# Moving one projection's units into later stages, and a new opening and closing of an expert stage, in a two-block transformer kernel on Trainium2

## What is computed

```python
# first block, mixer
proj = h @ w_in                       # split in columns: fq fk fv f_logit nq kc vc ... merge_logit
k_cmp, v_cmp = compress_kv(kc, vc)    # blocks of 32 tokens, stride 16, a two-layer MLP with gelu
y_fox = fox_attention(fq, fk, fv, log_f)
y_nsa = nsa_attention(nq, k_cmp, v_cmp, k_slc, v_slc, k_win, v_win, gates)
g = sigmoid(merge_logit)              # (tokens, 2 branches, 1024)
up = einsum('bsnc,ncd->bsnd', stack([y_fox, y_nsa]), w_branch)
merged = sum(g * up, axis=2);  h = h + merged @ w_out
# then 128 retrieved experts per token ("PEER"), rmsnorm
# second block: a gated delta rule mixer, then 16 experts that each choose 32 tokens
probs = softmax(xn @ router_w);  gate, idx = top_k(probs.T, 32)
xg = xn[idx]
y = (silu(xg @ w_gate[e]) * (xg @ w_up[e])) @ w_down[e] * gate
out = rmsnorm(h + scatter_add(y, idx))
```

## Time and profile before

| | us |
|---|---|
| median of 3 runs (lowest to highest) | 2330.33 (2324.06 to 2330.75) |
| profiled execution, time | 2327.65 |
| profiled execution, span from first to last instruction | 2325.9 |
| mean granted TensorE clock | 0.831 of 2.4 GHz |

### The profile page before, as it was taken

How to read it: one execution, slowest core, us unless ns; L and a number is a source line. 1 busy time by engine, 2 the same in 40 slices (tenths; PEclk the granted TensorE clock), 3 DMA queues, 4 the chain that set the end, 5 groups by cost and what they waited for, 6 DMA issues and landing times. The chain is left out here.

```text
span 2325.9 us, 22733 instructions
## 1 busy us (share of the span) xinstructions
PE 1733.6 (75%) x8678; PEld 871.0 (37%) x8678; DVE 756.1 (33%) x1643; ACT 438.6 (19%) x915; POOL 288.9 (12%) x297
## 2 busy tenths in 40 slices
PE   6997887987877778859788867666666666666675
PEld 6975687433333333329687631111111111111111
DVE  3425327876767666543464220000000000000001
ACT  4414223222212222224411020000000000000000
POOL 0000002433343333400051000000000000000000
PEclk9987998999899998989888777777777777787777
DMA  5530248999999999965000369999999999999996
GB/s 205 179 132 17 73 138 330 420 420 420 420 420 420 420 420 420 420 256 211 1 1 1 127 253 420 420 421 420 421 420 421 420 421 420 420 420 420 421 420 273
DMA packets 111080, 738.63 MB, mean 318 GB/s; under 512 B 13856, under 2 KB 15136, under 8 KB 27040
## 3 DMA queue, kind: packets, MB, share of 16 engines
q1 hardware_dynamic: 73856, 469.14, 50.0%
q0 software_dynamic: 36864, 268.45, 27.8%
q10 hardware_dynamic: 288, 0.08, 0.0%
HBM read 736.58 MB, written 1.05 MB: 317 GB/s over the span
## 5 line engine op out<-in xcount | busy, mean ns | idle before, releaser
L886 PE MATMUL ps<-arena 128*128 128x512 f32 x768 | 390.1, 661 | 132.0 <-ACT arena L947 132.0
L1898 PE MATMUL ps<-arena,xe 128*32 128x512 f32 x2048 | 353.7, 792 | 169.0 <-DMA arena<-in_experts_in 168.8
L1944 DVE TENSOR_TENSOR low<-low,ps 128x512 f32<-128x512 f32 x16 | 11.0, 687 | 890.4 <-PE ps L1898 890.4
L886 PEld LDWEIGHTS ps<-arena 128*128 128x128 f32 x768 | 156.0, 209 | 357.6 <-issue 188.6
L1030 DVE CUSTOM_DVE_ANT_0 arena<-arena,ps 128x1024 f32<-128x1024 f32 x192 | 231.9, 1218 | 113.5 <-DMA arena<-in_peer,arena 109.0
L833 POOL DMA_INDIRECT arena<-in_peer,arena x192 | 182.0, 948 | 692.8 <-DVE arena L1022 364.7
L1912 PE MATMUL ps<-arena,hT 128*32 128x512 f32 x1024 | 182.0, 811 | 102.2 <-DMA arena<-in_experts_down 90.5
L1898 PEld LDWEIGHTS ps<-arena,xe 128*32 128x32 f32 x2048 | 50.5, 122 | 461.7 <-DMA arena<-in_experts_in 419.6
L1912 PEld LDWEIGHTS ps<-arena,hT 128*32 128x32 f32 x1024 | 26.2, 127 | 240.5 <-DMA arena<-in_experts_down 213.3
L947 ACT ACTIVATE arena<-ident,arena 128x128 f32<-128x128 f32 x256 | 81.8, 390 | 122.1 <-DVE arena L1039 120.6
L333 PE MATMUL ps<-first_h_parts,first_w_parts 128*128 128x256 f32 x816 | 100.3, 286 | 5.3 <-DVE first_h_parts L298 4.3
(11 more groups left out here) (352 smaller groups left out, 1984.1 us busy)
## 6 DMA issues: line engine op xcount, KB each, us to landing
arena<-in_experts_in SPq DMA_DIRECT2D x256, 1024.0 KB, 26.9
arena<-in_experts_down SPq DMA_DIRECT2D x128, 1024.0 KB, 26.9
ring<-in_stream SPq DMA_DIRECT2D x80, 512.0 KB, 3.5
arena<-in_stream SPq DMA_DIRECT2D x14, 1024.0 KB, 7.5
arena<-in_peer,arena POOLq DMA_INDIRECT x192, 27.1
h<-in_x SPq DMA_DIRECT2D x1, 1024.0 KB, 5.1
arena<-in_sel SPq DMA_DIRECT2D x1, 1024.0 KB, 5.7
arena<-in_subkeys SPq DMA_DIRECT2D x2, 512.0 KB, 5.0
```

The source lines that it names most:

```text
L886: last = nc.tensor.matmul(ps[:, 4 + 2 * t + half, :], diag[:, n % DIAGS, :], slot(n)[:, D + half * BANK:D + (half + 1) * BANK], start=firs ...
L1898: last = nc.tensor.matmul(ps[32 * j:32 * (j + 1), 4 + r // KB, :], xe[:, k, :], w[:, j * BANK:(j + 1) * BANK], start=(k == 0), stop=(k == ...
```

## The change

**Merge gates.** The group of 16 units leaves the projection. The stream of weights after the projection is now mixed (`MIXED`): the eight compression pieces c0 to c7 and the 16 gate pieces m0 to m15. Six gate units run in the compression stage, between its pieces, and ten in attention, one in each of the steps 0, 1, 3, 4, 6, 7, 9, 10, 12 and 13, right behind the scores. ACT still makes the high parts, GpSimd instead of DVE makes the low parts, and two units share PSUM bank 7, from which ACT copies the pair (`gate_keep`) before the next pair may start. The Sigmoid comes in the merge block, eight activations on ACT. To free bank 7, the values of attention and of the compression's second layer move into bank 6. DVE has no gate unit's work any more.

```diff
-G_CMP, G_BRANCH, G_OUT, G_WQ, G_PEER = 40, 48, 56, 64, 80
+MIXED = ("c0 c1 m0 c2 c3 m1 c4 c5 m2 c6 c7 m3 m4 m5 m6 m7 m8 m9 m10 m11 m12 m13 m14 m15").split()
+G_MIXED, G_BRANCH, G_OUT, G_WQ, G_PEER = 24, 48, 56, 64, 80
+G_CMP = [G_MIXED + MIXED.index(f"c{i}") for i in range(8)]
+G_GATE = [G_MIXED + MIXED.index(f"m{i}") for i in range(16)]
+EARLY_GATES = 6
+G_ATT = G_GATE[EARLY_GATES]
...
     front(T, "mix", 0, ring, 0, [("F", 9, pieces(proj, 0, 9), ACT.Copy),
-                                 ("F", 8, pieces(proj, 9, 17), ACT.Sigmoid),
                                  ("T", 3, vdst, ACT.Copy)], small, refill, xs=T.arena[:, -NT * D:].rearrange("p (t d) -> p t d", t=NT))
...
+    def gate_split_high(act, u):
+
+        ring.arrived(act, G_GATE[u])
+        if u >= 2:
+            act.wait_ge(gate_done, u - 1)
+        nc.scalar.activation(gate_parts(u)[0], gate_raw(u), ACT.Copy).then_inc(gate_high, 1)
+
+    def gate_split_low(pool, u):
+
+        pool.wait_ge(gate_high, u + 1)
+        high, low = gate_parts(u)
+        nc.gpsimd.tensor_tensor(low, gate_raw(u), high.bitcast(F32), ALU.subtract).then_inc(gate_low, 1)
+
+    def gate_unit(pe, u):
+
+        if u >= 2 and u % 2 == 0:
+            pe.wait_ge(gate_kept, u // 2)
+        pe.wait_ge(gate_low, u + 1)
+        wh, wl = gate_parts(u)
+        for k in range(KB):
+            for m, (w, x) in enumerate(((wh, 0), (wl, 0), (wh, 1))):
+                last = nc.tensor.matmul(ps[:, 7, (u % 2) * S:(u % 2 + 1) * S], w[:, k, :], T.parts[:, x, k, :],
+                                        start=(k == 0 and m == 0), stop=(k == KB - 1 and m == 2))
+                if k == 0 and m == 0:
+                    last.then_inc(ring.used, 1)
+        last.then_inc(gate_done, 1)
...
+    def gate_keep(act, pair):
+
+        act.wait_ge(gate_done, 2 * pair + 2)
+        at = MERGE + 2 * pair
+        nc.scalar.activation(proj[:, at:at + 2, :].rearrange("p b s -> p (b s)"), ps[:, 7, :], ACT.Copy).then_inc(gate_kept, 1)
...
+        @block.gpsimd
+        def _(pool):
+            for u in range(EARLY_GATES + 2):
+                gate_split_low(pool, u)
...
+            rotate(0)
+            rotate(1)
             pe.wait_ge(kb_ready, 5)
...
+            compress(0)
+            compress(1)
+            gate_unit(pe, 0)
+            rotate(2)
+            compress(2)
+            compress(3)
+            gate_unit(pe, 1)
+            rotate(3)
+            compress(4)
+            compress(5)
+            gate_unit(pe, 2)
+            compress(6)
+            compress(7)
+            gate_unit(pe, 3)
...
             link = T.link(act, "act", T.chain_act)
+            gate_split_high(act, 0)
             nc.scalar.activation(gates[:, :, :], ps[:, 5, 0:48].rearrange("p (t c) -> p t c", t=NT), ACT.Sigmoid).then_inc(gates_ready, 1)
...
+            gate_split_high(act, 1)
+            gate_split_high(act, 2)
+            act.wait_ge(ring.used, G_CMP[3] + 1)
+            nc.scalar.activation(hsum[:, 0, :], ps[:, 2, 0:P], ACT.Copy).then_inc(hsum_ready, 1)
+            gate_keep(act, 0)
+            gate_split_high(act, 3)
+            act.wait_ge(ring.used, G_CMP[7] + 1)
+            nc.scalar.activation(hsum[:, 1, :], ps[:, 3, 0:P], ACT.Copy).then_inc(hsum_ready, 1)
+            gate_split_high(act, 4)
+            gate_keep(act, 1)
+            gate_split_high(act, 5)
             for j in range(2):
                 act.wait_ge(hid_ps, j + 1)
                 for grp in range(2):
                     nc.scalar.activation(hid[:, j, grp, 0:NCMP], ps[:, 4 + j, 16 * grp:16 * grp + NCMP], ACT.Gelu).then_inc(hid_ready, 1)
+            gate_split_high(act, 6)
+            gate_keep(act, 2)
+            gate_split_high(act, 7)
...
+    late = {3 * p + i: EARLY_GATES + 2 * p + i for p in range(5) for i in range(2)}
...
+        @block.gpsimd
+        def _(pool):
+            for u in range(EARLY_GATES + 2, 16):
+                gate_split_low(pool, u)
...
         def _(pe):
+            def gate(n):
+                if n in late:
+                    gate_unit(pe, late[n])
...
+            def gate(n):
+                p = n // 3
+                if p >= 5:
+                    return
+                u = EARLY_GATES + 2 * p + 2
+                if n % 3 == 1 and u < 16:
+                    gate_split_high(act, u)
+                if n % 3 == 2:
+                    gate_keep(act, u // 2 - 1)
+                    if u < 16:
+                        gate_split_high(act, u + 1)
+
+            stages(exps, None, evacuate, output, also=gate)
...
+        @block.scalar
+        def _(act):
+            for c in range(4):
+                for n in range(2):
+                    nc.scalar.activation(gate_of(c, n), gate_of(c, n), ACT.Sigmoid).then_inc(gate_open, 1)
```

```diff
+            sync.dma_start(gain_f, A["norm_final_2"]).then_inc(o_gain, 16)
             with sync.Fori(1, NEXP // 2) as pair:
                 for q in range(PAIR):
                     load(q, pair)
+            for t in range(NT):
+                sync.wait_ge(o_normed[t], 1)
+                sync.dma_start(T.out[t * P:(t + 1) * P, :], h[:, t, :]).then_inc(o_stored, 16)
+            sync.wait_ge(o_stored, 16 * NT)
...
+                def combine(half):
+                    pe.wait_ge(y_ready, 2 * e + half + 1)
+                    pe.wait_ge(og_ready, e + 1)
+                    for t in range(NT):
+                        last = nc.tensor.matmul(ps[:, 2 * t + half, :], og[:, t * P:(t + 1) * P], yb[:, half * BANK:(half + 1) * BANK],
+                                                start=opening, stop=closing, skip_group_check=True)
+                        if closing:
+                            last.then_inc(out_ps, 1)
...
-                    i, half = r // 2, r % 2
+                    half, i = r // 4, r % 4
...
+                    if r == 5:
+                        combine(0)
+                combine(1)
+
+            expert(0, 0, opening=True)
+            expert(0, 1)
+            with pe.Fori(1, NEXP // 2 - 1) as pair:
                 expert(pair, 0)
                 expert(pair, 1)
-
-            for b in range(4):
-                last = nc.tensor.matmul(ps[:, b, :], zeros[:, 0:P], zeros[:, :], start=False, stop=True, skip_group_check=True)
+            expert(NEXP // 2 - 1, 0)
+            expert(NEXP // 2 - 1, 1, closing=True)
...
-                act.wait_ge(ring.used, used(PER, e))
-                nc.scalar.activation(yb, ps[:, 6:8, :].rearrange("p b c -> p (b c)"), ACT.Copy).then_inc(y_ready, 1)
+                for half in range(2):
+                    act.wait_ge(ring.used, used(2 * KB + 4 * (half + 1), e))
+                    nc.scalar.activation(yb[:, half * BANK:(half + 1) * BANK], ps[:, 6 + half, :], ACT.Copy).then_inc(y_ready, 1)
...
+            nc.scalar.activation(ssq[:, 6:7], tokid[:, 0:1], ACT.Sqrt)
+            for half in range(2):
+                for t in range(NT):
+                    cols_h = slice(half * BANK, (half + 1) * BANK)
+                    act.wait_ge(h_ready, 2 * half + t + 1)
+                    nc.scalar.activation(junk, h[:, t, cols_h], ACT.Square,
+                                         accum_out=ssq[:, 2 * half + t:2 * half + t + 1]).then_inc(o_squares, 1)
+                    act.wait_ge(o_squares, 2 * half + t + 1)
+            act.wait_ge(o_mean, 1)
+            nc.scalar.activation(ss[:, 2:4], ss[:, 2:4], ACT.Sqrt).then_inc(o_root, 1)
+            act.wait_ge(o_gained, 2)
+            act.wait_ge(o_recip, 1)
+            nc.scalar.activation(h[:, 1, :], gained, ACT.Copy, scale=ss[:, 3:4]).then_inc(o_normed[1], 1)
...
+            for half in range(2):
+                for t in range(NT):
+                    cols_h = slice(half * BANK, (half + 1) * BANK)
+                    dve.wait_ge(out_ps, 2 * half + t + 1)
+                    nc.vector.tensor_tensor(h[:, t, cols_h], h[:, t, cols_h], ps[:, 2 * t + half, :], ALU.add).then_inc(h_ready, 1)
```

## The result

The changed kernel takes 2305.22 us (median, 2302.82 to 2309.59) where the kernel before, run beside it, takes 2327.49 (2324.06 to 2330.75): a ratio of 0.9912, 95% interval 0.9898 to 0.9926. That is 22 us less, 20.5 in the two profiled spans (2325.9 and 2305.4); the forecast was 33. The range held it, and two thirds of the forecast gain arrived.

The account below looks back on a forecast made before the run. PE bounds the projection and the weight stream the experts; compression and attention have free PE. Terms -47.2 + 17.0 + 10 + 0 - 3.6 + 1.2 - 10.4 = -33.0 off the 2330.3 us median gave 2297.3 us, range 2281 to 2315.

Parts of the forecast that it names:

- Projection, -47.2: Projection stage: 16 gate units leave the path, 46.2 us, and one PE stall of 0.96 us goes with them.
- Compression, +17: Compression stage: six added gate units and new waits, less filled idle and a better clock, lengthen it by 17 us.
- 17.3 + 1.5 + 2.5 + 2.7 - 5 - 2: Compression's sum: six units, waits ahead of units 1 and 3, stage end, filled waits, better clock; 17.0 us.
- -5: Compression: gate units fill PE's existing waits for the ring (3.0 us) and for DVE (2.0 us).
- The end's +2.7: End of compression: pair copy, high and low part 7 take 3.9 us where 1.2 us of key rotation stood.
- Attention, +10: Attention stage: ten added units, clock 0.90 and 10 us of idle left give 90.9 us against 80.8.
- Merge, 0: Merge stage: eight Sigmoids and a table load, 6.1 us on idle ScalarE beside PE's first pieces, cost nothing.
- Opening, -3.6 + 1.2: Start of expert stage: dropping zero matmuls moves the stream 3.6 us forward; the final gain's load within it adds 1.2.
- Closing, -10.4: End of expert stage: half copies, split scatter, norm and stores after the last weight piece end 10.4 us earlier.
- Rival 1: Compression and attention: idle takes the units, +7 and attention no longer than before, clock near 1; 2277 us, chance 0.13.
- Rival 2: Compression and attention: GpSimd's low parts hold DVE's normalisation and rotations, 18 us in all; 2315 us, chance 0.16.
- Rival 3: Compression and attention: clock stays low, neutral at a mean of 0.69, 2340 us at 0.65; chance 0.05.

Follow-up runs that it names:

- e4: Changed kernel with ScalarE copying a finished gate pair ahead of the step's exponentials in attention instead of behind them; 2297.2 us, ratio 0.9857 to the kernel before.
- e1: First block of the changed kernel with the expert stage of the kernel before; 2318.1 us, ratio 0.9951 to the kernel before.
- e7: Changed kernel with the last norm's gain loaded ahead of the expert stage instead of within the weight stream; 2299.6 us, ratio 0.9885 to the kernel before.
- e8: Changed kernel with pair's copy first, compression's low parts on VectorE, unit 7's split in attention and gain loaded early; 2283.8 us, ratio 0.9823.
- e9: The changed kernel run again without any edit, on the second chip; 2305.9 us, ratio 0.9904 to the kernel before.
- e6: Changed kernel with unit 7's high and low part at the start of attention instead of the end of compression; 2296.8 us, ratio 0.9878.
- e10: Changed kernel with the first half's combine behind an expert's eighth down piece instead of its sixth; 2306.2 us, ratio 0.9911 to the kernel before.
- e12: e8 with attention's low parts on VectorE too, so GpSimd does nothing in the first block; 2292.3 us, ratio 0.9842 to the kernel before.
- e5: Changed kernel with the compression stage's eight low parts on VectorE instead of GpSimd; 2297.1 us, ratio 0.9880 to the kernel before.
- e3: Changed kernel with compression's gate units 0 and 1, then 2 and 3, ordered in pairs; 2306.6 us, ratio 0.9904 to the kernel before.
- e11: e8 with the compression's gate units in pairs as in e3; 2284.9 us, ratio 0.9811 to the kernel before.

## Why the prediction was right, and where not

The mechanism was right: 16 units leave the projection, a part of them falls into idle time of two later stages, the new waits stand where they were named, and the experts open and close sooner. Four terms were mis-sized: the waits in compression, the pair's copy in attention, the stream's length and the final stores. Nearly all the errors lie on one side, so they do not cancel: the sum was 11 us too optimistic, and the range held the result by its width.

- **Projection, -47.2.** Measured -45.9, of which +0.75 is a later landing of the inputs. Right.
- **Compression, +17; measured +23.6.** Of "17.3 + 1.5 + 2.5 + 2.7 - 5 - 2": the two waits were 3.6 and 4.4 instead of 1.5 and 2.5, because I took the median landing of the earlier trace rows for a piece that is requested close to others. That median was weak by itself: the trace holds the landing of only two of the stage's eight transfers, 4.0 us for the one issued at 162.2 and 5.3 for the one at 167.3, and 4.6 is their middle. 5.3 us would have given 2.2 and 3.2, still short of the measured waits. The "-5" held for 3 only: the 2.0 us behind VectorE did not go but were replaced by 2.3 behind the additions that GpSimd's low part stretched. The clock gave 1.2 instead of 2. The end's +2.7 was about right (4.1 us of idle there now).
- **Attention, +10; measured +13.4.** The clock (0.91 for 0.90) was right and the busy time 2 us under the forecast, the idle time 5.4 over it. The step that failed is the sentence that the wait for the pair's copy falls "mostly in place of idle that I have just kept": it came on top. e4 took it out and got 8.1 us, clock behind the waits included, which leaves +5.3.
- **Merge, 0.** No change here: 65.3 us in both. Five of the twelve experiment traces have 66.9, for a reason told in the last section.
- **Opening, -3.6 + 1.2.** The first expert matmul came 14.4 us sooner, 5.7 more than the transposes. Over the twelve traces with this opening the mean is 4.8, while before and e1, with the old one, agree within 0.1; so the 3.6 are borne out in sign and rough size, not measured by themselves. The stream grew by 3.3 instead of 1.2: 1.7 goes with the gain load by e7 and its likes (1.3 in the spacing of the landings, as forecast), and about 1.5, a term that the prediction did not have, arises in one place near the end, from a cause that is not shown.
- **Closing, -10.4; measured -9.4**, the 1.0 being 1.2 more for the stores.

**Rival 1** (the idle takes the units) was too optimistic for the change as it is, and right on what the stages can hold: e8 has attention at 81.4 us.

**Rival 2** (GpSimd and VectorE in each other's way, 18 us) named L672 and the rotations. In the trace of the changed kernel and in e1, e7 and e9 no rotation was held. In e4 two were (2.72 and 2.30 us instead of 0.69), in e6 and e10 one each (1.51 and 1.00), with the same program up to there: whether they meet is an execution's own. No wait of TensorE is put down to them. One normalise was held as well (L765, 0.22 us of work):

```profile
188.11 2.38 POOL L448 TENSOR_TENSOR first_w_parts<-ring,first_w_parts 128x1024 fp32r<-128x1024 f32 x1 [2.84 <-ACT first_w_parts L442]
188.20 2.37 DVE L765 TENSOR_TENSOR arena<-arena,stat 128x60 f32<-128x60 f32 x1
```

It was held to the end of the low part, fully, but in only 1 of 16 steps, and e12 shows that attention is better off with these collisions than with its low parts in VectorE's row as placed there. The meeting that cost was the one I had not listed, the kb additions at the start of compression. So the mechanism is real, and its price in TensorE's waits came out at some 2 us plus the longer low parts themselves, not at 18. The Trainium skill's rule ("SBUF — State Buffer", section "Who interferes with whom"), that whoever issues second is blocked for the whole of the other, agrees with these rows: 2.37 us for 0.22. The first of the four kb additions does not fit it: issued 0.03 us behind a low part's start, it ran unheld (0.43 us), and the second one was held.

**Rival 3** (the clock stays low) is out: 0.87 and 0.91, where 0.69 would have been neutral.

The chances gave 0.92 to faster by over 0.3%, and it was faster by 0.9%.

## What to carry to other kernels

Work that is moved into idle time of a later stage brings its own feeding chain with it. Price that chain by the longest landing in the window, not the median, look how many landings that median rests on, and ask of each engine in it what stands ahead of it in program order: here one copy behind four exponentials cost 8 us, and low parts on the slower engine cost 3 to 11. And here the stage that waits directly for a helper wanted the fast engine for it, while the stage with a step of slack wanted the idle one; the same operation had its right place on VectorE in compression and on GpSimd in attention.

## What the hardware showed that I had not expected

VectorE's scaling of the maximum (L750, a tensor_scalar of 128 x 4 numbers with a single SBUF operand) was held by GpSimd too, while the reduction ahead of it, issued under the same low part, ran free:

```profile
182.92 2.35 POOL L448 TENSOR_TENSOR first_w_parts<-ring,first_w_parts 128x1024 fp32r<-128x1024 f32 x1 [8.08 <-ACT first_w_parts L442]
...
183.49 0.22 DVE L749 TENSOR_REDUCE stat<-arena 128x4 f32<-128x60 f32 x1
183.74 1.56 DVE L750 TENSOR_SCALAR stat<-stat 128x4 f32<-128x4 f32 x1
```

With no low part beside it the same instruction takes 0.17 us. It ended at 185.30, with the low part (185.27). ScalarE's exponentials wait for it. The same section of the Trainium skill says that a tensor_scalar can run in a mode that uses both ports and then contends, and that a tensor_reduce on trn2 cannot; both agree with these rows. I had kept the prediction to operations with two SBUF operands, and so had missed this one.

The second is how much the stage with many short waits varies: with one and the same program compression took 48.2 to 52.2 us from execution to execution, by landings between 3.2 and 6.6 us and by whether a unit behind a wait took 3.1 us or 4.4 to 5.5. In e5 a unit behind a wait of 2.30 us kept the full clock; in e3 one behind 2.26 us took 4.53. The merge stage shows it most cleanly, since nothing in it differs between the kernels with the moved units: TensorE waits 2.16 us, 30 us into the stage, and then goes on with matmuls. In e3, e4, e5, e8 and e12 the granted clock fell behind that wait (0.50 from 269.1 to 272.4 us in e4) and the stage took 66.9 us; in the others it stayed up (1.00 from 281.3 to 284.6 in the changed kernel) and the stage took 65.3. e11 and e12 have the same program in this stage and fall on different sides. What decides between them these rows do not show.
